# A full-row contraction for attention scores, with the other head's query rows held at zero

## What is computed

```python
xn = rms_norm(x, norm_mix_g)
z  = xn @ w_in                       # columns [B | C | h | q | k | v], 512 each
y_conv = short_gated_conv(B, C, h)   # 3 taps
q, k = rms_norm(q, q_gain), rms_norm(k, k_gain)      # per head, 8 heads of 64
scores = einsum("qd,kd->qk", q, k) * 64 ** -0.5 + rel_bias  # a query chunk of 64 sees 9 chunks of keys
y_attn = softmax(scores) @ v
x = x + concat(group_norm(y_conv), group_norm(y_attn)) @ w_out
x = x + relu(rms_norm(x) @ w_mlp_in) ** 2 @ w_mlp_out
```

## Time and profile before

| | |
|---|---|
| runs | 1225.32, 1231.07, 1230.14 us; median 1230.14 |
| the profiled execution | 1227.32 us, of which the span from first to last instruction is 1225.5 us |
| busy in the span | PE 1164.6 us (95%), DVE 777.3, POOL 610.1, ACT 529.7 |
| mean granted TensorE clock | 0.983 |

### The profile page before, as it was taken

One profiled execution on the slowest core, in us unless ns is written; L12 is line 12 of the kernel. 1 busy time (PEld: TensorE's weight loads), 2 busy tenths in 40 slices (PEclk: granted clock), 3 DMA queues, 4 the chain that ended last, 5 costly groups with the idle time before them and its releaser, 6 DMA issues.

```text
span 1225.5 us, 14666 instructions
## 1 busy us (share of the span) xinstructions
PE 1164.6 (95%) x5368; PEld 946.2 (77%) x5368; DVE 777.3 (63%) x867; ACT 529.7 (43%) x827; POOL 610.1 (50%) x331
## 2 busy tenths in 40 slices
PE   5999999998999998899799999999998999999998
PEld 4878877876887686688678888888876888888886
DVE  6566866785677668744534344453448787676887
ACT  5554443446344545321444544545453333343330
POOL 4211230223032203001478787877869789697892
PEclk9999988998999899999999999999999999999999
DMA  7310110111011041311135444444386534435324
GB/s 224 106 35 18 55 34 17 34 36 51 0 51 36 1 172 52 138 53 69 60 104 172 155 138 157 154 160 148 138 292 249 198 129 161 166 112 196 122 87 155
DMA packets 98512, 135.81 MB, mean 111 GB/s; under 512 B 8072, under 2 KB 52112, under 8 KB 98456
## 3 DMA queue, kind: packets, MB, share of 16 engines
q1 hardware_dynamic: 95104, 131.13, 31.5%
q10 hardware_dynamic: 3352, 3.94, 1.1%
HBM read 97.27 MB, written 39.34 MB: 111 GB/s over the span
## 4 chain that ended last, share of the span: by engine, by line
PE 83%; DVE 9%; issue 2%; DMA 2%; POOL 1%; ACT 1%; SPq 0%; DVEq 0%; ACTq 0%; POOLq 0%
PE PJ L1399 18%; PE PJ L1646 8%; PE SC L1646 8%; PE OS L1646 7%; PE PJ L1680 6%; PE PT L1680 6%; PE SC L1680 6%; PE OS L1680 6%; PE PJ L1472 5%; PE SC L1430 4%; DVE sq L954 3%; PE OS L1454 2%; PE PT L1441 2%; DVE sql L944 2%; DMA gB<-in_norm_mlp_g 1%
## 5 line engine op out<-in xcount | busy, mean ns | idle before, releaser
L1399 PE MATMUL PJ<-actT,wsl 128*128 128x512 f32 (+1 forms) x1176 | 313.5, 410 | 0.0
L1399 PEld LDWEIGHTS PJ<-actT,wsl 128*128 128x128 f32 x1176 | 214.3, 195 | 50.4 <-issue 5.7
L562 POOL TENSOR_TENSOR ring<-b,ring 128x1024 fp32r<-128x1024 f32 x48 | 137.7, 2877 | 37.8 <-ACT ring L883 37.7
L1309 DVE TENSOR_TENSOR ring<-hraw,ring 128x1024 fp32r<-128x1024 f32 x56 | 151.0, 2731 | 3.8 <-ACT ring L878 3.8
L484 POOL CAST wsl<-raw 128x1024 fp32r<-128x1024 f32 x24 | 27.0, 1127 | 240.7 <-PE PJ L1399 225.8
L878 ACT ACTIVATE ring<-hraw 128x1024 fp32r<-128x1024 f32 x56 | 59.2, 1057 | 134.4 <-PE OS L1680 63.6
L520 POOL TENSOR_TENSOR w1a<-w1r,w1a 128x512 fp32r<-128x512 f32 x32 | 50.5, 1580 | 122.0 <-ACT w1a L815 122.0
L1646 PE MATMUL OS<-actT,w1a 128*128 128x512 f32 x384 | 93.1, 391 | 2.0 <-POOL w1a L520 2.0
L664 ACT ACTIVATE prob<-prob,negm 128x640 f32<-128x640 f32 (+4 forms) x64 | 44.6, 696 | 114.3 <-DVE negm L1024 114.1
L1680 PE MATMUL PJ<-ring 128*128 128x512 f32 x336 | 82.4, 395 | 6.0 <-POOL ring L562 4.4
L1646 PEld LDWEIGHTS OS<-actT,w1a 128*128 128x128 f32 x384 | 72.3, 189 | 17.3 <-POOL w1a L520 2.2
(11 more groups left out here) (182 smaller groups left out, 2224.9 us busy)
## 6 DMA issues: line engine op xcount, KB each, us to landing
hraw<-hidd SPq DMA_DIRECT2D x56, 512.0 KB, 3.6
w1r<-in_w_mlp_in SPq DMA_DIRECT2D x16, 1024.0 KB, 6.1
b<-in_w_mlp_out SPq DMA_DIRECT2D x16, 1024.0 KB, 6.4
hidd<-hs SPq DMA_DIRECT2D x64, 256.0 KB, 2.0
raw<-in_w_in SPq DMA_DIRECT2D x24, 512.0 KB, 3.6
hidd<-h SPq DMA_DIRECT2D x48, 256.0 KB, 2.2
xin<-in_x SPq DMA_DIRECT2D x8, 512.0 KB, 8.5
woraw<-in_w_out SPq DMA_DIRECT2D x8, 512.0 KB, 7.4
```

The lines of the kernel that those rows point to most:

```text
L562: nc.gpsimd.tensor_tensor(duo(n)[1][LO], W2_SRC[name][:, 2 * d:2 * d + 2], duo(n)[1][HI].bitcast(F32), ALU.subtract).then_inc(s["wl2_done" ...
L1309: vec.tensor_tensor(duo(n)[0][LO], hraw[:, n % HRING], duo(n)[0][HI].bitcast(F32), ALU.subtract).then_inc(s["hl2_done"], 1)
L1399: last = mm(PJ[:, g % 2, cols], wsl[:, w % NSLOT, a, k], actT[:, b, k, c], start=(r == 0), stop=(r == 3 * KD - 1))
```

## The change

The scores contract over all 128 rows. `kT` is used as it is, with both heads on its rows. Of q there are now two copies with 128 rows each, one per head, in which the other head's rows are zero: for head 0 `qT` with rows 64 to 127 zeroed once at the start by DVE; for head 1 `qz`, which lies in two planes (3 and 7) of the region of `xin` and `ymix` that are not written before the last iteration, with rows 0 to 63 zeroed once by POOL. POOL may do that only when PE has transposed all of `xin`, and the code puts it between the weights of k and those of v, for which POOL's first iteration is written out apart from the loop (`weights(0, True)`). Every operation that wrote q's HI or LO part for 128 rows is now two operations of 64 rows each.

```diff
--- before.py
+++ after.py
@@ -80,6 +80,8 @@
 
         xin = nc.alloc_sbuf_tensor_at("xin", [P, NT, DM], F32, offset=RB)
         ymix = nc.alloc_sbuf_tensor_at("ymix", [P, NT, KD, P], F32, offset=RB)
+        qz = nc.alloc_sbuf_tensor_at("qz", [P, NT, KD, P], F32R, offset=RB)
+        QZ = (NPAIR - 1, 2 * NPAIR - 1)
         put, top = plan(RB)
         u2 = put("u2", [P, 2, HALF], F32)
         u4 = put("u4", [P, HALF], F32)
@@ -164,6 +166,14 @@
         def half(n):
             return slice(n * HALF, (n + 1) * HALF)
 
+        HEADS = (slice(0, HD), slice(HD, P))
+
+        def q_plane(hh, hl, n, rows):
+
+            if hh == 0:
+                return qT[rows, hl, half(n)].rearrange("p (t c) -> p t c", c=P)
+            return qz[rows, 4 * n:4 * n + 4, QZ[hl], :]
+
         def col(t):
 
 
@@ -189,7 +199,7 @@
 
         names = """
         g_in prm_in rel_in rev_out skew_out bias_in g_again out_written
-        consts act_warm passed mask_set masks_ok prm_g rev_built
+        consts qt_zero qz_zero act_warm passed mask_set masks_ok prm_g rev_built
         ssx_done sdx_done rsx_done xs_done tr_done xhi_done xlo_done
         whi_done w_ready proj_done ones_done vt_done sc_done pt_done pv_done us_done uq_done oq_done ot_done
         prm_ready halo_done sql_done sqlk_done qlo_done rs_done zn_done rsc_done znc_done qklo_done vlo_done
@@ -474,7 +484,7 @@
             nc.gpsimd.affine_select(out=ident[:, :], in_=ident[:, :], compare_op=ALU.not_equal, fill=1.0, base=0,
                                     pattern=[[-1, P]], channel_multiplier=1).then_inc(s["consts"], 1)
 
-            with pool.Fori(0, NPAIR) as it:
+            def weights(it, first):
                 for w in range(NW):
                     sl = w % NSLOT
                     pool.wait_ge(raw_in[w % 2], it * (NW // 2 * 16) + 16 * (w // 2 + 1))
@@ -491,8 +501,25 @@
                         nc.gpsimd.tensor_tensor(sql[:, 1], sq[:, 1], sqh[:, 1].bitcast(F32), ALU.subtract
                                                 ).then_inc(s["sqlk_done"], 1)
                         pool.wait_ge(s["hi_done"], it * 4 + 1)
-                        nc.gpsimd.tensor_tensor(qT[:, LO, half(0)], zs[:, 0], qT[:, HI, half(0)].bitcast(F32),
-                                                ALU.subtract).then_inc(s["qlo_done"], 1)
+                        pool.wait_ge(s["sqlk_done"], it + 1)
+                        for hh, rows in enumerate(HEADS):
+                            if hh:
+                                pool.wait_ge(s["qlo_done"], it * 2 + 1)
+                            nc.gpsimd.tensor_tensor(q_plane(hh, LO, 0, rows),
+                                                    zs[rows, 0].rearrange("p (t c) -> p t c", c=P),
+                                                    q_plane(hh, HI, 0, rows).bitcast(F32), ALU.subtract
+                                                    ).then_inc(s["qlo_done"], 1)
+                        pool.wait_ge(s["qlo_done"], it * 2 + 2)
+                    if w == 1 and first:
+                        pool.wait_ge(s["tr_done"], NT)
+                        pool.wait_ge(s["w_ready"], 2)
+                        for slot in QZ:
+                            nc.gpsimd.memset(qz[HEADS[0], :, slot, :].bitcast(F32), 0.0).then_inc(s["qz_zero"], 1)
+                        pool.wait_ge(s["qz_zero"], len(QZ))
+
+            weights(0, True)
+            with pool.Fori(1, NPAIR) as it:
+                weights(it, False)
             for k in POOL_WO:
                 pool.wait_ge(s["wohi_done"], k + 1)
                 nc.gpsimd.tensor_tensor(wo[:, k, LO, :].rearrange("p (a c) -> p a c", a=2), woraw[:, 2 * k:2 * k + 2, 0:HALF],
@@ -622,7 +649,7 @@
             def take(it, n):
 
                 if n == 2:
-                    act.wait_ge(s["qlo_done"], it + 1)
+                    act.wait_ge(s["qlo_done"], it * 2 + 2)
                 if n == 3:
                     act.wait_ge(s["qklo_done"], it * 3 + 1)
                 g = QKGROUP[n]
@@ -637,7 +664,12 @@
 
             def qk_hi(it, n):
                 act.wait_ge(s["zn_done"], it * 4 + (n + 1))
-                act.activation((qT, kT)[n % 2][:, HI, half(n // 2)], zs[:, n % 2], ACT.Copy).then_inc(s["hi_done"], 1)
+                if n % 2 == 0:
+                    for hh, rows in enumerate(HEADS):
+                        op = act.activation(q_plane(hh, HI, n // 2, rows), zs[rows, 0].rearrange("p (t c) -> p t c", c=P), ACT.Copy)
+                else:
+                    op = act.activation(kT[:, HI, half(n // 2)], zs[:, 1], ACT.Copy)
+                op.then_inc(s["hi_done"], 1)
 
             def v_copy(it, n):
 
@@ -909,6 +941,7 @@
             vec.memset(bias[0:HD, :, BANDW - CHUNK:BANDW], NEG).then_inc(s["masks_ok"], 1)
             vec.memset(bias[HD:P, :, 0:CHUNK], NEG).then_inc(s["masks_ok"], 1)
             vec.memset(ones[:, :].bitcast(F32), 0.0).then_inc(s["mask_set"], 1)
+            vec.memset(qT[HEADS[1], :, :].bitcast(F32), 0.0).then_inc(s["qt_zero"], 1)
             dve.wait_ge(s["mask_set"], 1)
             vec.memset(ones[0:HD, 0:HD].bitcast(F32), 1.0).then_inc(s["mask_set"], 1)
             vec.memset(ones[HD:P, HD:P].bitcast(F32), 1.0).then_inc(s["mask_set"], 1)
@@ -962,10 +995,14 @@
                                          ALU.mult, ALU.mult).then_inc(s["zn_done"], 1)
 
             def qk_lo(it, n):
-                dst = (qT, kT)[n % 2]
                 dve.wait_ge(s["hi_done"], it * 4 + (n + 1))
-                vec.tensor_tensor(dst[:, LO, half(n // 2)], zs[:, n % 2], dst[:, HI, half(n // 2)].bitcast(F32),
-                                  ALU.subtract).then_inc(s["qklo_done"], 1)
+                if n % 2 == 0:
+                    for hh, rows in enumerate(HEADS):
+                        op = vec.tensor_tensor(q_plane(hh, LO, n // 2, rows), zs[rows, 0].rearrange("p (t c) -> p t c", c=P),
+                                               q_plane(hh, HI, n // 2, rows).bitcast(F32), ALU.subtract)
+                else:
+                    op = vec.tensor_tensor(kT[:, LO, half(n // 2)], zs[:, 1], kT[:, HI, half(n // 2)].bitcast(F32), ALU.subtract)
+                op.then_inc(s["qklo_done"], 1)
 
             def conv_gate(it, n):
 
@@ -1415,9 +1452,12 @@
             def score(it, u):
                 t, hh = u // 2, u % 2
                 nb = keys(u)
-                hp = slice(hh * HD, (hh + 1) * HD)
+                if u < 2:
+                    pe.wait_ge(s["qlo_done"], it * 2 + (u + 1))
                 if u == 0:
-                    pe.wait_ge(s["qlo_done"], it + 1)
+                    pe.wait_ge(s["qt_zero"], 1)
+                if u == 1:
+                    pe.wait_ge(s["qz_zero"], len(QZ))
                 if u in (0, 8):
                     pe.wait_ge(s["qklo_done"], it * 3 + (1 if u == 0 else 3))
                 if u:
@@ -1427,7 +1467,7 @@
                 for c0, c1 in ((at, min(HALF, at + nb * P)), (HALF, at + nb * P)):
                     if c0 < c1:
                         for n, (a, b) in enumerate(PASSES):
-                            last = mm(SC[:, c0:c1], qT[hp, a, t * P:(t + 1) * P], kT[hp, b, k0 + c0:k0 + c1],
+                            last = mm(SC[:, c0:c1], q_plane(hh, a, t // 4, slice(0, P))[:, t % 4], kT[:, b, k0 + c0:k0 + c1],
                                       start=(n == 0), stop=(n == 2))
                 last.then_inc(s["sc_done"], 1)
 
```

## The result

The changed kernel takes **1199.08 us** in the median of 4 runs (1198.77 to 1199.29), the kernel before 1227.8 in the 4 runs beside them (1225.32 to 1231.07). The ratio is 0.9761, with a 95% interval of 0.9738 to 0.9783: 2.4% faster.

What follows compares the result with a forecast made beforehand. PE was taken to bound attention, except where DVE ends a stretch. Savings of 25.0 less 3.5 (lost in waits), 2.4 (stall), 2.0 (clock) and 0.7 (unit 3) gave 16.4 us: 1210.9, forecast as 1212 us, range 1203 to 1221.

Steps and rivals of the forecast that it cites:

- The row changes: Around each attention unit's scores, 128-to-64-row switches lose 0.395 us; 64 units give 25.0 us, 3.5 of it not coming through.
- The second place: From a unit's first to second score matmul, 0.105 us lost (0.28 against 0.175), one of four places of loss.
- Rival 3: The 0.395 us at the scores has another cause, as tile and bank changes, and stays; 1232.4 us; chance 0.04.
- rival 2: DVE becomes the pace in attention units with inversions, swallowing half the saving; 1220 to 1222 us; chance 0.13.
- Rival 1: Saving comes with little given back: no clock fall at the start, short memsets, shorter boundaries; about 1203 us; chance 0.13.
- Rival 4: Full-row loads of the score matmuls are no longer hidden, 55 us more less the 25; 1257 us; chance 0.02.
- The start: POOL's memsets take 2.0 us and stall PE 2.4 us for v's weights; low clock behind costs 2.0 us.
- I take 0 for the three boundaries: Split POOL operations at iteration boundaries may add or spare DVE collisions (L1061); net 0, range -3 to +5 us.
- Unit 3: PE's waits for sql stay at 2.2 us or grow to 3; collisions of POOL and DVE cost 0.7 in all.
- The four old stalls in unit 3 stay, so their clock falls stay: Low clock behind unit 3's stalls is unchanged by the edit; +/-3 us kept in the range for where falls lie.

Runs made afterwards that it cites:

- the tiny matmul: Rows alone plus one overwritten 64-row, 32-column matmul ahead of each unit's scores; 1225.12 us, ratio 0.9972.
- the late memsets: Changed kernel with POOL's two memsets moved behind v's weights and q's LO part; 1196.88 us, ratio 0.9744.
- Split alone: Kernel before with q's HI and LO of the first half each written by two 64-row operations, scores unchanged; 1222.3 us, ratio 0.9949.
- rows alone: Kernel before with score matmuls reading all 128 rows, mixing heads; no copies, zeroed rows, memsets or split operations; 1201.02 us, ratio 0.9766.
- all but the rows: Changed kernel with each score matmul back on its head's 64 rows, memsets and split operations kept; 1221.36 us, ratio 0.994.
- before shifted: Kernel before with eight discarded 512-column matmuls ahead of the first iteration; 1227.0 us, ratio 0.9988.
- middle on 64 rows: Changed kernel with the middle one of each three score matmuls on its head's 64 rows; 1233.2 us, ratio 1.0029.
- rows shifted: Rows alone with eight discarded 512-column matmuls ahead of the first iteration; 1199.83 us, ratio 0.9772.
- the best kernel: Changed kernel with the late memsets and DVE's prm copy and small memset moved to unit 1, sum of squares in its old place; 1188.1 us, ratio 0.9667.
- the later sum of squares: PE's sum of squares for n = 3 moved from unit 3 to unit 4: in the kernel before 1210.28 us, with the late memsets 1198.76 us.
- The fourth batch: Every attention fill contracted over rows 0 to 63 only: in the kernel before 1446.66 us, in the changed kernel 1451.96 us.
- sum of squares later: The late memsets with PE's sum of squares for n = 3 moved from unit 3 to unit 4; 1198.76 us, ratio 0.9754.
- copy later: Sum of squares later, with DVE's prm copy and small memset moved from ahead of the first softmax step to unit 1; 1190.33 us, ratio 0.9691.

## Why the prediction was wrong, point by point

**The row changes: the mechanism right, the size near.** 25.0 us of gaps were forecast, of which 3.5 would be lost in waits. The gaps fell by 22.2 (27.4 less 5.2). Of that, 18 to 20 us reached the time: 1221.36 less 1199.08 and 1229.09 less 1201.02, the two pairs that differ in the rows alone, are 22.3 and 28.1, of which some 4 and 8 are low clock by the estimate below. The unit became 0.38 shorter, 0.395 was forecast, but not where I had put it. In the means of 31 wide units, from the transpose to the scores it is 0.17 shorter (forecast 0.11), from the first to the second score 0.02 (forecast 0.105), from the scores to the fills 0.09 (0.08) and between the first two fills 0.10 (0.10). The second place had little to do with the rows: 0.26 of its 0.28 stay with full rows. That the first was undersized by about as much is luck. The price per change held under three tests: 0.19 where I added changes alone, 0.16 around the tiny matmul, 0.17 in the change itself (22.2 over 128). It belongs to the change of rows and not to the 64-row matmul. By the rule on the Trainium skill's page TensorEngine Tiling (Array Packing), Key Properties, a new tiling mode drains TensorE; the runs fit that, and give it this price. Rival 3 is out, and rival 2 as well: PE's waits didn't grow, 28.4 to 27.2. Rival 1 (1203) came nearest in time, but of its reasons only the boundaries came true. Rival 4 is out too: the score matmuls, full-row and back to back, run at full pitch.

**The start: right.** The memsets took 1.84 (forecast 2.0), the stall 2.41 (2.4). Low clock came behind it, for 3.4 us, of which a window shows 3.2:

```profile
44.00:47.20 3.20, 3.20 (x9) 2.44 (x8) 0.09 (x1) 0.00 (x0) 0.00 (x0) 0.50 0.48 141
```

The start grew by 4.04, so the clock took some 1.6 (forecast 2.0). But the late memsets show that such a stall removed is not all returned.

**"I take 0 for the three boundaries": mis-sized.** They gave back some 4 us, a little more than the 3 that I had as the most. That DVE is spared its collision, which I kept as a possibility, is what happens. Boundary of the kernel after, timeline of DVE and POOL:

```profile
253.51 0.69 DVE L1098 TENSOR_TENSOR osq<-on 128x512 f32<-128x512 f32 x1
...
253.69 1.67 POOL L508 TENSOR_TENSOR qT<-zs,qT 64x512 fp32r<-64x512 f32 x1 [2.86 <-ACT qz L669]
```

```profile
261.73 2.35 POOL L496 TENSOR_TENSOR wsl<-raw,wsl 128x1024 fp32r<-128x1024 f32 x1
261.74 2.36 DVE L1189 COPY prm<-prm_all 128x6 f32 x1 [0.73 <-ACT ymix L711]
```

L1098, the counterpart of L1061, begins 0.18 ahead of POOL and is not held. Before, PE waits three times at each boundary (waits of PE in the kernel before: us in total, times, longest):

```profile
PE SC L1430 <- DVE kT L967: 2.2, 3, 0.8
PE SC L1430 <- DVE negm L1024: 2.0, 3, 0.8
PE OS L1467 <- DVE on L1070: 1.7, 3, 0.6
```

That is 5.9 us. After, one wait is left at each, of 0.34, 2.20 and 0.24 us; the one of 2.20 is in the boundary of the second fence above, where the copy is held. Split alone is worth 5.7 us, of which about 4 remain without the low clock, and 3.8 us of waits are left there, both for the copy. The changed kernel has about 4 us from its boundaries too: without the low clock it is 1.7 us faster than rows alone, though it pays the new stall of 2.4. I had costed the boundary by one known collision, and had asked neither which of the two starts first nor which short DVE operation POOL would meet next. The Trainium skill's GPSIMD Engine Reference, Key points, says that GpSimd shares its SBUF interfaces with VectorE and contends with VectorE's instructions that have two SBUF inputs or run in a two-port mode; the runs agree, with 0.17 us alone and 2.3 behind a POOL start for the copy.

**Unit 3: the wait right, its clock wrong.** Timeline after, DVE and then PE (to the earlier trace rows):

```profile
280.69 2.81 DVE L994 SCALAR_TENSOR_TENSOR zs<-zs,gqk,sq 128x512 f32<-128x512 f32 x1
283.43 0.68 DVE L977 TENSOR_TENSOR sql<-sq,sqh 128x512 fp32r<-128x512 f32 x1
```

```profile
280.61 1.54 PE L1436 MATMUL PJ<-actT,wsl 128*128 128x512 f32 x6
284.23 0.49 PE L1449 MATMUL OS<-sqh,ones 128*128 128x512 f32 x1 [2.09 <-DVE sql L977]
```

L994 now collides instead of `sql`, and PE waits nearly as long as it did (2.09 us, where it was 2.21). **The step that failed is "The four old stalls in unit 3 stay, so their clock falls stay".** The stalls stayed, and the falls did not: behind the four stalls the profile before has 23.8 us of low clock, the profile after none, and over all kernels a stall has 4.3 us behind it with 64-row scores and 1.2 with full-row ones. One of them in the kernel after, the stall and then what follows, by windows:

```profile
175.90:178.00 2.10, 0.11 (x1) 0.00 (x0) 2.10 (x3) 0.60 (x1) 0.92 (x1) 1.00 0.00 0
178.20:185.00 6.80, 6.80 (x36) 5.78 (x37) 4.02 (x7) 6.01 (x9) 0.00 (x0) 1.00 0.25 73
```

36 matmuls in 6.8 us at full clock, where before 20 ran in as long at half. Rows alone, the same stall and what follows:

```profile
173.10:175.30 2.20, 0.15 (x1) 0.00 (x0) 2.20 (x3) 0.68 (x2) 0.94 (x1) 1.00 0.01 2
176.00:179.20 3.20, 3.20 (x11) 2.74 (x10) 0.57 (x2) 3.16 (x4) 0.00 (x0) 0.50 0.44 128
179.40:182.60 3.20, 3.20 (x20) 2.76 (x20) 2.47 (x4) 0.92 (x4) 0.00 (x0) 1.00 0.00 0
```

Split alone, scores on 64 rows:

```profile
186.50:188.70 2.20, 0.06 (x1) 0.00 (x0) 2.20 (x2) 1.76 (x2) 1.55 (x1) 0.99 0.00 0
188.80:195.40 6.60, 6.60 (x18) 4.84 (x19) 0.94 (x4) 2.68 (x4) 0.00 (x0) 0.50 0.27 79
```

The tiny 64-row matmul:

```profile
180.90:183.20 2.30, 0.21 (x1) 0.00 (x0) 2.30 (x2) 1.92 (x3) 1.71 (x1) 1.00 0.00 0
185.20:188.40 3.20, 3.20 (x11) 2.63 (x10) 0.64 (x3) 1.55 (x3) 0.00 (x0) 0.50 0.20 61
```

All kernels with that stall in unit 3 (1.9 to 2.2 us, four in each profile), by the length of low clock that begins within 5 us of the stall's start:

| scores | kernels | stalls | 6.8 us | 3.4 us | none | mean |
|---|---|---|---|---|---|---|
| 64 rows | before, all but the rows, split alone, before shifted | 16 | 9 | 2 | 5 | 4.3 |
| 128 rows with changes | tiny 64-row matmul, middle on 64 rows | 8 | 0 | 7 | 1 | 3.0 |
| 128 rows | after, rows alone, memsets late, rows shifted, the best kernel | 20 | 0 | 7 | 13 | 1.2 |

A fall is not certain: in one profile (all but the rows) stalls of 2.19 and 2.20 us are followed by 0 and 6.8 us. Over the kernels the order is plain. One more difference goes along with the rows: with changes a stall of the first three iterations is 2.18 to 2.23 us long, without them 2.07 to 2.09. It is not the reason. The kernels with the later sum of squares have longer stalls, eight of 2.41 to 2.56 us in unit 4, with full-row scores, and two are followed by 3.4 us and six by none. The fourth batch shows the cause by dose: with the fills on 64 rows the engine stays at 1.2 GHz through a hundred us in which it is hardly idle, with full-row scores or without. So shown is that 64-row scores bring more low clock, and that 64-row work in a large dose holds the clock low by itself. Not shown is which part of the 64-row scores does it, the contraction or the gaps of the changes. The tiny matmuls have almost no 64-row work and all of the changes, and the clock costs 16 us there, against 12 with rows alone and 20 before; one fall of 6.8 us lies in a boundary of theirs. So the gaps may well carry about half. Open as well is what ended the long stretches: from 342 us, with 64-row fills still in the work, the clock was full again.

**The size of it.** The mean time of a kernel's runs less its profile's time without the excess under low clock is my estimate of what the clock costs a kernel; it holds what falls behind the attention too. In us:

| scores | what the clock costs |
|---|---|
| 64 rows | before 20, split alone 18, before shifted 17, all but the rows 16; with no stall in unit 3 (the later sum of squares in the kernel before) 9 |
| 128 rows with changes | tiny 64-row matmul 16, middle on 64 rows 14 |
| 128 rows | after 12, rows alone 12, rows shifted 12, memsets late 12, sum of squares later 12; copy later 9, the best kernel 7 |

So of the clock's 11.3 us between the two profiles in the attention, some 8 belong to the kernels, and the rest to where the falls lay. The forecast misses 13 us: about 8 are this clock and 4 the boundaries; the row changes brought 2 to 3 less than forecast, and what is left is small terms and the spread of the runs.

**The range.** Its low end, 1203, added the boundary's gain, and no case for the clock on unchanged stalls beyond +/-3 us. The rows at hand had two stalls with 3.3 and 6.8 us of low clock behind them. These could have told me that the fall behind a stall is not a constant, and is itself something that the change may move.

## What to carry to other kernels

Count the places in PE's list where the number of contracted rows changes, at 0.16 to 0.19 us each here, before you count columns. Padding the short contraction with zero rows cost a matmul nothing here (0.175 us for 384 columns either way), and removed both the gap and part of the low clock behind stalls. A stall that an edit leaves alone is not a constant: the low clock behind it changed with the rows of the scores around it. And the same edit (the later sum of squares) was worth 18 us in one kernel and nothing in the other, since the other had DVE as the bound there. Where POOL and DVE work at the same time, ask of each short DVE operation which of the two starts first (0.17 against 2.3 us here), and move the short one out of the way: that and the late memsets were worth 11 us more.

## What the runs showed of the hardware that I had not expected

- Contraction over half of the rows can hold TensorE at 1.2 GHz though it is busy for 83.93 of 84 us: 229 matmuls, with 512-column products 0.427 us apart, against 0.23.
- A DVE copy of 128x6 that begins behind a POOL step of two SBUF inputs ends with it: in five profiles it began 9 to 99 ns behind eight times, took 2.28 to 2.37 us each time, and ended 0.03 us after POOL. A few ns decide: four that began 0 to 5 ns behind took 0.17. The 128x512 operation with two inputs that begins 0.09 or 0.18 ahead of POOL takes its own 0.69.
- Not every DVE operation is held: in the kernel before, a reciprocal of 128x1 that began 0.08 us behind such a POOL step took 0.14.
- The clock's record can be missing: 1.00 stood in windows in which 512-column fills were 0.427 us apart, as where 0.50 is recorded.
